# A depthwise convolution's taps moved from ScalarE and GpSimd to TensorE, as 128x32 weights over shifted copies

## What is computed

```python
proj = h @ w_in                                   # 1024 -> 3 x 1024
a, b, gate = jnp.split(proj, [CONV_WIDTH, 2 * CONV_WIDTH], axis=-1)
glu = a * jax.nn.sigmoid(b)
conv = lax.conv_general_dilated(                  # 31 taps, causal, one filter per channel
    glu, dw_w, window_strides=(1,), padding=[(CONV_K - 1, 0)],
    dimension_numbers=('NWC', 'WIO', 'NWC'), feature_group_count=CONV_WIDTH)
cf = conv + dw_b
cn = (cf - mu) * lax.rsqrt(var + EPS) * ln_g + ln_b      # LayerNorm over the channels
y = jax.nn.silu(cn) * jax.nn.silu(gate)
return y @ w_out
```

## Time and profile before

| | us |
|---|---|
| three runs | 1124.29, 1125.66, 1127.17 |
| the profiled execution | 1125.93 |
| its span, first to last instruction | 1124.1 |

### The profile page before, as it was taken

How to read it: one execution, slowest core, us unless ns; L and a number is a source line. 1 busy time by engine, 2 the same in 40 slices (tenths; PEclk the granted TensorE clock), 3 DMA queues, 4 the chain that set the end, 5 groups by cost and what they waited for, 6 DMA issues and landing times.

```text
span 1124.1 us, 12285 instructions
## 1 busy us (share of the span) xinstructions
PE 1033.6 (92%) x4847; PEld 824.7 (73%) x4847; DVE 584.4 (52%) x768; ACT 468.5 (42%) x765; POOL 170.0 (15%) x131
## 2 busy tenths in 40 slices
PE   3899999997999999999999979989898899979897
PEld 2677677886788888888888868767677667657676
DVE  5436665235744234333344463366556397777853
ACT  3325562135533334134123354234355557556541
POOL 2200101000000000000000000022000189886300
PEclk8999999998999999999999999989999799999989
DMA  6532102034221252233224214302033222210301
GB/s 213 73 122 76 38 1 76 1 113 150 76 76 75 75 187 75 75 109 116 76 75 149 76 38 132 141 1 75 2 136 120 68 76 76 75 54 27 145 1 75
DMA packets 55823, 93.91 MB, mean 84 GB/s; under 512 B 2581, under 2 KB 23958, under 8 KB 55638
## 3 DMA queue, kind: packets, MB, share of 16 engines
q1 hardware_dynamic: 53648, 90.61, 23.3%
q10 hardware_dynamic: 2118, 2.52, 1.6%
HBM read 90.76 MB, written 2.36 MB: 83 GB/s over the span
## 4 chain that ended last, share of the span: by engine, by line
PE 55%; DVE 8%; ACT 4%; issue 3%; POOL 1%; DMA 1%; SPq 0%; DVEq 0%; POOLq 0%; ACTq 0%
PE acc L702 17%; PE acc L703 17%; PE acc L704 16%; DVE wlr L1768 2%; ACT wh L1362 2%; DVE psT L2113 1%; POOL pacc L1295 1%; PE psT L861 1%; DMA wl<-in_c_w_in_dram 1%; PE ps L861 1%; PE ps L993 1%; DVE rt L1795 1%; DVE act_lo L1812 1%; ACT junk L1391 1%; PE psT L978 1%
## 5 line engine op out<-in xcount | busy, mean ns | idle before, releaser
L1768 DVE TENSOR_TENSOR wlr<-wl,wh 128x2048 fp32r<-128x2048 f32 (+1 forms) x66 | 149.9, 2276 | 96.4 <-ACT wh L1362 96.4
L702 PE MATMUL acc<-act_hi,wh 128*128 128x512 f32 x464 | 187.9, 405 | 1.7 <-DVE act_lo L1812 1.4
L704 PE MATMUL acc<-act_hi,wlr 128*128 128x512 f32 x464 | 182.3, 393 | 0.0
L703 PE MATMUL acc<-act_lo,wh 128*128 128x512 f32 x464 | 182.1, 392 | 0.0
L1362 ACT ACTIVATE wh<-wl 128x2048 fp32r<-128x2048 f32 (+1 forms) x66 | 123.7, 1880 | 61.2 <-DMA wl<-in_w_up_dram 35.1
L702 PE MATMUL acc<-wh,act_hi 128*128 128x512 f32 x320 | 131.3, 410 | 19.0 <-DVE act_lo L1738 7.6
L703 PE MATMUL acc<-wlr,act_hi 128*128 128x512 f32 x320 | 127.6, 399 | 0.0
L704 PE MATMUL acc<-wh,act_lo 128*128 128x512 f32 x320 | 127.6, 399 | 0.0
L1295 POOL TENSOR_TENSOR pacc<-pacc,prod 128x512 f32<-128x512 f32 x80 | 117.5, 1469 | 28.6 <-ACT prod L1644 16.1
L702 PEld LDWEIGHTS acc<-act_hi,wh 128*128 128x128 f32 x464 | 88.4, 191 | 21.7 <-DVE act_lo L1812 1.8
L703 PEld LDWEIGHTS acc<-act_lo,wh 128*128 128x128 f32 x464 | 88.3, 190 | 19.1 <-issue 1.7
(11 more groups left out here) (221 smaller groups left out, 1536.8 us busy)
## 6 DMA issues: line engine op xcount, KB each, us to landing
wl<-in_w_up_dram SPq DMA_DIRECT2D x16, 1024.0 KB, 6.3
wl<-in_w_down_dram SPq DMA_DIRECT2D x16, 1024.0 KB, 6.3
raw<-in_w_in_dram SPq DMA_DIRECT2D x18, 512.0 KB, 4.8
wl<-in_a_w_in_dram SPq DMA_DIRECT2D x8, 1024.0 KB, 6.2
wl<-in_c_w_in_dram SPq DMA_DIRECT2D x16, 512.0 KB, 6.2
wl<-in_w_out_dram SPq DMA_DIRECT2D x4, 1024.0 KB, 6.2
wl<-in_ab_w_out_dram SPq DMA_DIRECT2D x4, 1024.0 KB, 7.4
wl<-in_c_w_in_dram SPq DMA_DIRECT2D x4, 1024.0 KB, 6.4
```

What stands on the lines that cost most here:

```text
L702: pe.matmul(dst, hi, x_hi, start=first, stop=False)
L703: pe.matmul(dst, hi, x_lo, start=False, stop=False)
L704: return pe.matmul(dst, lo, x_hi, start=False, stop=last)
L1768: dve.tensor_tensor(wlr[slot][:, kk, cols], wl[slot][:, kk, cols], wh[slot][:, kk, cols].bitcast(F32), ALU.subtract).then_inc(wlo_done, 1)
```

## The change

Of the 31 taps TensorE takes 16, VectorE 15 (8 in `y_tap`, summed in SBUF with the bias; 7 in `x_tap`, on top of TensorE's sum in PSUM), and ScalarE and GpSimd none. TensorE's 16 are four passes m of four matmuls c. One has weights of 128 rows x 32 columns: the rows are 4 taps x 32 channels, the columns the 32 channels of group c, and its output the partitions 32c to 32c+31. Its moving tile is `shifted[:, t % 2, c, :]`, in which partitions 32j to 32j+31 hold the channels of group c moved by j tokens; pass m reads it from column 4m on. SP makes `shifted` from `glu` with 16 DMAs per conv tile (`shift`), each 32 partitions x 524 elements (67 KB). The weights `tapw` are made by GpSimd, one multiplication per conv tile, from the taps in a new arrangement (`ptaps`, four small DMAs and a transpose) and a 0/1 pattern. `conv_taps(t)` stays where it was in TensorE's order, except t = 7, which moves one tile later; `turn_conv` moves later. ScalarE's and VectorE's hand-written orders are written anew.

Apart from the convolution, GpSimd takes the low weight halves of N_UP, N_GA, N_AB (at the three passages) and N_CO0 from VectorE (`lo_following`). At s = 0 and 1 ScalarE makes the high halves at b = 0 and 1.

```diff
-PE_TAPS = 4
-DVE_TAPS = 16
-ACT_TAPS = TAPS - DVE_TAPS - PE_TAPS
-PRODUCTS = ACT_TAPS + 1
-COPY_AT = ACT_TAPS - 2
+PE_TAPS = 16
+PASSES = PE_TAPS // 4
+Y_TAPS = 8
+X_TAPS = TAPS - PE_TAPS - Y_TAPS
...
+        ysum = at("ysum", [P, 2, TOK], arena + 52 * KB)
...
+        shifted = cC("shifted", [P, 2, 4, SHIFTED])
...
+        tapw = at("tapw", [P, 2, 4 * PASSES, 32], sq_off + KB)
...
-                    sp.wait_ge(un_done, 3 * NBLK)
-                    gain(lng[:, :], a["c_ln_g_2"][0], ln_in)
-                    gain(lnb[:, :], a["c_ln_b_2"][0], ln_in)
+            conv_w = a["c_dw_w_2"]
+            sp.dma_start(tap_rows[:, :], conv_w[0, :, 0, :]).then_inc(taps_in, 16)
+            for m in range(PASSES):
+                sp.dma_start(tap_sets[32 * m:32 * m + 32, :].rearrange("p (j c) -> p j c", j=4),
+                             bass.AP(conv_w.tensor, 4 * m * D, [[32, 32], [D, 4], [1, 32]])).then_inc(taps_in, 16)
+            sp.dma_start(pattern[:, :], a["shapes"][:, 4 * P + TOK + 64:4 * P + TOK + 96]).then_inc(taps_in, 16)
+
+            def shift(t):
+
+                sp.wait_ge(evD_done, evacs_before(TILE_AT[N_AB, 0], "D") + t + 1)
+                if t >= 2:
+                    sp.wait_ge(petap_done, t - 1)
+                for c in range(4):
+                    for j in range(4):
+                        sp.dma_start(shifted[32 * j:32 * j + 32, t % 2, c, :],
+                                     glu[32 * c:32 * c + 32, t % 4, j:j + SHIFTED]).then_inc(shift_in[t % 2], 16)
+
+            load_chunk(N_AB + 0, c_in, ((0, 0, CW), (CW, D + 0, CW)))
+            load_chunk(N_AB + 1, c_in, ((0, 256, CW), (CW, D + 256, CW)))
+            sp.wait_ge(un_done, 3 * NBLK)
+            gain(lng[:, :], a["c_ln_g_2"][0], ln_in)
+            gain(lnb[:, :], a["c_ln_b_2"][0], ln_in)
+            shift(0)
+            load_chunk(N_AB + 2, c_in, ((0, 512, CW), (CW, D + 512, CW)))
+            shift(1)
+            shift(2)
+            load_chunk(N_AB + 3, c_in, ((0, 768, CW), (CW, D + 768, CW)))
+            shift(3)
+            shift(4)
             load_chunk(N_G0, c_in, ((0, 2 * D, 512),))
+            shift(5)
+            shift(6)
             load_chunk(N_G1, c_in, ((0, 2 * D + 512, 512),))
+            shift(7)
             load_chunk(N_CO0, a["c_w_out_2"][0], ((0, 0, 512),))
...
 
             def conv_taps(t):
 
-                pe.wait_ge(evD_done, evacs_before(TILE_AT[N_AB, 0], "D") + t + 1)
-                pe.wait_ge(diag_done, PE_TAPS * (t + 1))
-                if t >= 2:
-                    pe.wait_ge(conv_done, t - 1)
-                for m in range(PE_TAPS):
-                    j = TAPS - PE_TAPS + m
-                    last = pe.matmul(vacc(t, 0), diag[:, t % 2, m, :], glu[:, t % 4, j:j + TOK],
-                                     start=m == 0, stop=m == PE_TAPS - 1)
+                pe.wait_ge(shift_in[t % 2], 16 * 16 * (t // 2 + 1))
+                pe.wait_ge(tapw_done, t + 1)
+                if t >= 3:
+                    pe.wait_ge(conv_done, t - 2)
+                for m in range(PASSES):
+                    for c in range(4):
+                        last = pe.matmul(xsum(t)[32 * c:32 * c + 32, :], tapw[:, t % 2, 4 * m + c, :],
+                                         shifted[:, t % 2, c, 4 * m:4 * m + TOK], start=m == 0, stop=m == PASSES - 1)
...
             pe.wait_ge(ob_done, 4)
             for k in range(KT):
-                last = pe.transpose(ps6[:, k * TAPS:(k + 1) * TAPS], tap_rows[:, k * P:(k + 1) * P],
-                                    ident[0:TAPS, 0:TAPS])
-            last.then_inc(taps_ps, 1)
+                pe.transpose(ps6[:, k * TAPS:(k + 1) * TAPS], tap_rows[:, k * P:(k + 1) * P], ident[0:TAPS, 0:TAPS])
+            pe.transpose(ps6[:, KT * TAPS:KT * TAPS + P], tap_sets[:, :], ident[:, :]).then_inc(taps_ps, 1)
             turn_block(2, 2)
...
@@ -1180,11 +1197,11 @@
                     channel_tile(N_AB + i, m, 1)
                     if (i, m) in after:
                         turn_conv(after[i, m])
...
             for i in range(2):
                 for b in range(NBLK):
                     token_tile(N_G0 + i, b, 0)
-                    if i == 0 and b == 0:
+                    if i == 0 and b == 1:
                         conv_taps(KT - 1)
                     token_tile(N_G0 + i, b, 1)
                     if (i, b) in after:
...
+
+            def lo_following(n):
+
+                for piece in range(2):
+                    kk, cols = slice(4 * piece, 4 * piece + 4), slice(0, chunk_width(n))
+                    pool.wait_ge(whi_done, piece_count(n, piece))
+                    pool.wait_ge(wlo_done, piece_count(n, piece) - 1)
+                    pool.tensor_tensor(wlr[n % 2][:, kk, cols], wl[n % 2][:, kk, cols],
+                                       wh[n % 2][:, kk, cols].bitcast(F32), ALU.subtract).then_inc(wlo_done, 1)
...
+            lo_following(N_UP)
+            lo_following(N_GA)
             pool.wait_ge(wtile_done, CHUNK_END[N_GA - 1])
             pool.memset(uu[:, :, 0:UPAD], 0.0).then_inc(upad_set, 1)
             for step in STEPS_OF[1]:
                 mixer_step_pool(1, step)
+            lo_following(N_AB)
...
+                if t >= 2:
+                    pool.wait_ge(petap_done, t - 1)
+                pool.tensor_tensor(tapw[:, t % 2, :, :].rearrange("p (m c) n -> p m c n", m=PASSES),
+                                   pattern.rearrange("p (m c n) -> p m c n", m=1, c=1).to_broadcast([P, PASSES, 4, 32]),
+                                   ptaps[:, :, 4 * t:4 * t + 4].rearrange("p m (c n) -> p m c n", n=1)
+                                   .to_broadcast([P, PASSES, 4, 32]), ALU.mult).then_inc(tapw_done, 1)
+            lo_following(N_CO0)
...
-                    if b in (1, 2):
-                        hi(following, b - 1)
+                    if b in ((1, 2) if s == 2 else (0, 1)):
+                        hi(following, b - (s == 2))
...
+            sigmoid(1)
+            sigmoid(2)
+            hi(N_AB + 2, 0)
+            hi(N_AB + 2, 1)
+            sigmoid(3)
+            conv_out(0)
+            sigmoid(4)
+            hi(N_AB + 3, 0)
+            hi(N_AB + 3, 1)
+            conv_out(1)
+            sigmoid(5)
+            conv_out(2)
+            sigmoid(6)
+            hi(N_G0, 0)
+            hi(N_G0, 1)
+            conv_out(3)
+            sigmoid(7)
+            conv_out(4)
+            gate_out(N_G0, 0)
+            hi(N_G1, 0)
+            conv_out(5)
+            hi(N_G1, 1)
+            gate_out(N_G0, 1)
+            gate_out(N_G0, 2)
+            conv_out(6)
+            gate_out(N_G0, 3)
+            gate_out(N_G1, 0)
+            hi(N_CO0, 0)
+            hi(N_CO0, 1)
...
-                    if b >= 2:
-                        lo(following, b - 2)
                     if b >= 1:
                         lo_turned(s, b - 1)
                     normed(s, b)
                 lo_turned(s, NBLK - 1)
+                dve.wait_ge(wlo_done, piece_count(following, 1))
...
                 if t >= 4:
-                    dve.wait_ge(prod_done, PRODUCTS * (t - 3))
-                    dve.wait_ge(petap_done, t - 3)
+                    dve.wait_ge(shift_in[t % 2], 16 * 16 * (t // 2 - 1))
+                    dve.wait_ge(x_step, X_TAPS * (t - 3))
                 dve.tensor_tensor(glu[:, t % 4, CPAD:], acc[:, TILES[e][2], :], sg[:, t % 2, :], ALU.mult)\
                    .then_inc(evD_done, 1)
...
+            def y_tap(t, i):
+
+                src, sums = glu[:, t % 4, PE_TAPS + i:PE_TAPS + i + TOK], ysum[:, t % 2, :]
+                scale = taps[:, t, PE_TAPS + i:PE_TAPS + i + 1]
+                if i == 0:
                     dve.wait_ge(evD_done, evacs_before(TILE_AT[N_AB, 0], "D") + t + 1)
-                if earlier:
-                    dve.wait_ge(tap_step, DVE_TAPS * t + earlier[-1] + 1)
-                elif which == 0:
+                    if t >= 2:
+                        dve.wait_ge(conv_done, t - 1)
+                    ins = dve.tensor_scalar(sums, src, scale, vec[:, V_DWB + t:V_DWB + t + 1], ALU.mult, ALU.add)
+                else:
+                    dve.wait_ge(y_step, Y_TAPS * t + i)
+                    ins = dve.scalar_tensor_tensor(out=sums, in0=src, scalar=scale, in1=sums, op0=ALU.mult, op1=ALU.add)
+                ins.then_inc(y_step, 1)
+
+            def x_tap(t, i):
+
+                j = PE_TAPS + Y_TAPS + i
+                if i == 0:
                     dve.wait_ge(petap_done, t + 1)
-                elif t >= 1:
-                    dve.wait_ge(prod_done, PRODUCTS * (t - 1) + COPY_AT + 1)
-                if which == 1 and not earlier:
-                    ins = dve.tensor_scalar(sums, src, taps[:, t, m:m + 1], vec[:, V_DWB + t:V_DWB + t + 1],
-                                            ALU.mult, ALU.add)
                 else:
-                    ins = dve.scalar_tensor_tensor(out=sums, in0=src, scalar=taps[:, t, m:m + 1], in1=sums,
```

(72 more changed lines are left out.)

85 lines of the change are left out of this document (17 added, 68 removed).

## The result

The kernel with the change takes 1211.2 us in the median (1210.2, 1211.2 and 1213.8; a fourth execution, disturbed, took 1561.1 at a mean granted clock of 0.64 and is left out of every comparison) against 1125.6 before: a ratio of 1.0763, interval 1.0743 to 1.0783. The profiled execution took 1211.16 us, 85.2 more than that of before. It is slower and inside the range, as forecast, but 23 us over the forecast's value of 1188 and at the upper end of its own range, 1157 to 1213.

What follows compares the result with a forecast made beforehand. TensorE, 92% busy, bounds the kernel, so only its pauses and slow stretches can be won. The convolution stage's +53.1 us and the passages' +9.3 sum to +62.4, giving 1188 us; range 1152 to 1225, own range 1157 to 1213.

Steps and rivals of the forecast that it cites:

- waits, t = 0, 2, 4, 6: Convolution stage, even conv tiles: TensorE's taps wait 6.7 us each for shifted copies landing 9.3 us after the tile's end.
- waits, t = 1, 3, 5: Convolution stage, odd conv tiles: copies queue behind a 2 MB weight chunk, so TensorE waits 8.4 us each.
- wait, t = 7: Convolution stage, last conv tile: taps stand a tile and a half later, so 2.5 us of waiting remain.
- taps and lower clock: Convolution stage: eight taps of 3.9 us, 31.2 us, plus 1.95 us of lower clock after each of seven waits, 13.7 us.
- passages: Three passages: GpSimd's low halves and VectorE block each other; +4.3, +1 and +4 us, sum +9.3, bounds -7 and +13.
- The issue: SP's shifted copies: issues 0.40 us apart, 6.0 us for the fifteen ahead of the last, bounds 0.35 to 0.50.
- One after another: Rival on the taps: 32-column matmuls run serially, 13.8 instead of 3.9 us, total 1267 us; sequential or paired columns 0.14.
- two together: Milder rival on the taps: matmuls run in pairs, 6.9 us, total 1212 us; chance 0.14 shared with fully sequential columns.
- The rule about row groups: Skill's rule for the taps: a weight load overlaps running matmuls only when its row group differs; implies the serial 1267 us.
- Issuing hides behind the data: Rival on the copies: they land as one transfer in 6.4 us, even waits 2.9 us shorter; 1176 or 1168 us; chance 0.12.
- The passages gain: Rival at the passages: no blocking between VectorE and GpSimd, -7 us instead of +9.3, total 1172 us; chance 0.10.
- Faster: Rival in the convolution stage: copies land before TensorE reaches the taps; stage 176.5 us, total 1104 us; chance 0.06.

Runs made afterwards that it cites:

- The second queue: Changed kernel with eight of each conv tile's sixteen copies issued by ScalarE's queue instead of SP: 1189.3 us, ratio 1.0567 to the kernel before.
- the forms: Changed kernel plus series of SP DMAs differing in source, size and partitions: SBUF-to-SBUF issues 0.62 to 0.64 us apart, from DRAM 0.52; one execution 1206.5 us.
- the exchange of two loops: Changed kernel with the taps' matmuls ordered so that one channel group's four passes come one after another: 1250.4 us, ratio 1.1109 to the kernel before.
- smaller pieces: Changed kernel with each GpSimd low half at a passage cut into four 128x512 instructions: 1196.3 us; this part alone in the kernel before: 1120.8 us.
- Three further edits: Changed kernel with taps one tile later, copies on two queues and weight loads behind the copies, passages also put back: 1116.0 us, ratio 0.9914 to the kernel before.
- the passages put back: Changed kernel with low weight halves of N_UP, N_GA, N_AB back on VectorE and high ones at b = 1 and 2: 1204.5 us, ratio 1.0699.

## Why the prediction was right, and where it was off

By its own steps, each with its forecast and what was measured in the profiled execution:

| term, us | forecast | measured |
|---|---|---|
| waits, t = 0, 2, 4, 6 | 4 x 6.7 | 37.1 (8.99 to 9.57) |
| waits, t = 1, 3, 5 | 3 x 8.4 | 32.6 (9.74 to 11.48) |
| wait, t = 7 | 2.5 | 3.9 |
| taps and lower clock | 31.2 + 13.7 | 47.9 |
| `conv_out(7)` to the next product | 13.7 | 13.8 |
| the rest of the stage | 131.6 | 132.9 |
| stage | 244.7 | 268.2 |
| passages | +9.3 | +8.5 |

**The issue, mis-sized.** Of the 23.5 us that the stage took beyond its forecast, 19 are waits. The step that failed is "I take 0.40, 6.0 us for fifteen, and keep 0.35 to 0.50": fifteen issues took 9.5 us, 0.63 apart, above the upper bound. The landing went the other way, 2.0 instead of 2.6 us. From `gated(0)` at 899.26 to the taps at 911.51 are 12.25 us against 9.3 forecast, and TensorE waited 9.57 instead of 6.7. The second queue and the forms confirm this price independently. The mistake was to take a price from one issue at the start of a series when a price between issues was wanted, and of another kind (DRAM to SBUF); the four and two weight loads of the earlier trace rows, 0.46 to 0.51 each, were nearer.

**Odd tiles.** The mechanism, copies queued behind 2 MB, exists, but in the changed kernel it was not what ended the waits of 11.48 and 11.39: 2.0 us of weight issues and 10.5 us of copies did. It showed only when the issue was halved, and then with 11.2 us, where I had worked out 8.4. There the copies came in last 13.9 us after the first weight issue, where 11 had been worked out from 349 GB/s and the full DMA engines gave 280. Both bounds were under-estimated, and that odd tiles wait longer was right for a reason that stood second in line.

**Clock and taps.** The granted clock answers to the 0.50 and 0.68 of the earlier trace rows: 0.50 is 1.2 GHz, the lower level, and TensorE had stood since 901.9.

```profile
905.00:910.00 5.00, 0.00 (x0) 0.00 (x0) 3.21 (x3) 0.00 (x0) 0.00 (x0) 0.71 0.44 107
910.00:915.00 5.00, 3.49 (x20) 0.87 (x24) 0.00 (x0) 0.00 (x0) 0.00 (x0) 0.50 0.11 27
915.00:920.00 5.00, 5.00 (x29) 2.24 (x22) 0.00 (x0) 0.00 (x0) 1.05 (x1) 0.77 0.02 3
```

Eight taps took 47.9 us. At full clock they take 3.64 each, 29.1 in all, so the clock cost 18.8, 1.6 to 2.9 and on average 2.35 for each of eight waits; I had 1.95 for seven and 3.9 for the taps. The taps were 2.1 us too dear in all and the clock 5.1 too cheap, so the two errors cancelled in part. t = 7, whose wait of 3.9 us cost as much clock as the long ones (6.08 us of taps), had been left out.

**The rivals.** *One after another* fell: four run together, by the bursts of weight loads and by the 3.64 us of the taps at full clock. The time alone could not have told this: *two together*, the milder form of that rival, gave 1212 us, nearly what was measured, with taps of 6.9 us of work. But one after another was a real condition, since the exchange of two loops costs 39 us. The rule about row groups that was named beside it ("TensorE: Matmul & The Clock Gate" of the Trainium skill, section "Part 3: Packing small matmuls — row/col tiling") would have kept every load apart from running matmuls here, as all four matmuls use all 128 rows. The trace doesn't agree with it: in the 6.10 us from 1103.50 the taps' matmuls are busy 6.08 us, and their weight loads, four at a time, take 1.31 us beside them. *Issuing hides behind the data* fell for the change and was turned round: data hid behind issuing. *The passages gain* fell for the change and holds with smaller pieces. *Faster*: its condition was a landing that is early enough for TensorE. Three further edits make it true, and the stage then takes 181.5 us, where that rival had 176.5.

**The passages.** By s, the net effects are +2.5, -0.5 and +5.5 us against +4.3, +1 and +4, with about +1 between them, and `un` and `rt` of 2.4 to 5.6 us. The sum of 8.5 in one profile agrees with 9.3 better than the single steps do, which is partly luck: kernels with the same code up to there differ by 4 us in where the stage starts, and the medians with the passages put back say 7. The mechanism, VectorE standing under GpSimd's halves, is what the rows show.

## What to carry over

A transfer that an engine waits for costs the number of its DMAs times the distance of their issues before it costs bytes: price it from several issues in a row, and put the consumer one stage later in the order before making the transfer faster. When a bound is halved, look for the next one at the same place, as the weights ahead of the copies here. An elementwise instruction for GpSimd that runs beside VectorE's chain should be short, since VectorE can wait for all of it.
